# Sample tokens' attention to cached keys: 16 rows, transposed keys, scores inside the input projection; a fifth head's products one unit later

## The reference, cut to what matters

```python
def swa_sample(q, k, v, buf, window, dil):
    ...
    kk = jnp.concatenate([buf[:, :, 0].astype(F32), k.astype(F32)], axis=1)
    vv = jnp.concatenate([buf[:, :, 1].astype(F32), v.astype(F32)], axis=1)
    idx = Wb + jnp.arange(T)[:, None] - dil * jnp.arange(J + 1)[None, :]
    ...
    s = jnp.einsum('nthd,ntjhd->nthj', q.astype(F32), kg) * (Dh ** -0.5)
    mx = jnp.max(s, axis=-1, keepdims=True)
    p = jnp.exp(s - mx)
    den = jnp.sum(p, axis=-1)
    o = jnp.einsum('nthj,ntjhd->nthd', p, vg) / den[..., None]
    lse = mx[..., 0] + jnp.log(den)
# in mixer: the three groups are merged by their denominators
    alpha = jax.nn.softmax(jnp.stack(lses, axis=2), axis=2)
    out_s = (jnp.stack(outs, axis=2) * alpha[..., None]).reshape(B, T, W_SW)
```

## Time and profile before

| | |
|---|---|
| median of 3 runs | 2053.05 us (2052.51 to 2056.39) |
| the profiled execution, its own time | 2051.47 us |
| its span in the profile | 2049.7 us |
| PE, DVE, ACT, POOL busy | 1768.1, 990.9, 697.4, 361.9 us |
| layer 0: projection's last tile moved out, prompt's attention done, `window_end` | at 230.1, 271.5, 314.6 us |
| layer 1: the same three points | at 1111.2, 1151.4, 1197.0 us |

### The profile page before, as it was taken

One profiled execution on the slowest core, in us unless ns is written; L12 is line 12 of the kernel. 1 busy time (PEld: TensorE's weight loads), 2 busy tenths in 40 slices (PEclk: granted clock), 3 DMA queues, 4 the chain that ended last, 5 costly groups with the idle time before them and its releaser, 6 DMA issues. The chain is left out here.

```text
span 2049.7 us, 34030 instructions
## 1 busy us (share of the span) xinstructions
PE 1768.1 (86%) x13616; PEld 1652.8 (81%) x13616; DVE 990.9 (48%) x1485; ACT 697.4 (34%) x1038; POOL 361.9 (18%) x226
## 2 busy tenths in 40 slices
PE   6999846659999999997999567494999999999994
PEld 6898714449999999997997254394999999999994
DVE  4575463544221122226663735434664574574484
ACT  4443414214222122234333143134343353353342
POOL 4002401014344344441005000013000000000021
PEclk9999956569999999999999665596999999999997
DMA  4211306312222222222113010115876776786792
GB/s 169 73 63 52 115 0 235 134 46 83 86 91 96 77 87 93 99 77 73 63 53 125 0 62 0 45 64 214 278 242 236 269 257 227 258 276 217 249 332 68
DMA packets 68700, 270.71 MB, mean 132 GB/s; under 512 B 11189, under 2 KB 11925, under 8 KB 67773
## 3 DMA queue, kind: packets, MB, share of 16 engines
q1 hardware_dynamic: 61152, 242.05, 34.2%
q10 hardware_dynamic: 3772, 18.36, 2.6%
q0 software_dynamic: 3648, 8.53, 1.2%
HBM read 252.55 MB, written 36.29 MB: 141 GB/s over the span
## 5 line engine op out<-in xcount | busy, mean ns | idle before, releaser
L1651 PE MATMUL psum<-xg,xhi 128*128 128x320 f32 x1408 | 376.9, 310 | 0.9 <-issue 0.4
L1653 PE MATMUL psum<-xg,xlo 128*128 128x256 f32 x1408 | 375.3, 281 | 0.0
L1651 PEld LDWEIGHTS psum<-xg,xhi 128*128 128x128 f32 x1408 | 265.5, 189 | 2.9 <-issue 2.6
L583 POOL TENSOR_TENSOR wlo<-wraw,whi 128x1024 fp32r<-128x1024 f32 (+1 forms) x82 | 209.9, 2562 | 318.2 <-ACT whi L719 318.2
L1653 PEld LDWEIGHTS psum<-xg,xlo 128*128 128x128 f32 x1408 | 264.7, 188 | 0.0
L1122 PE MATMUL psum<-xnh,whi 128*128 128x260 f32 x1120 | 235.2, 292 | 31.1 <-POOL xnl L636 13.8
L719 ACT CAST whi<-wraw 128x1024 fp32r<-128x1024 f32 (+1 forms) x130 | 140.7, 1085 | 308.5 <-DMA wraw<-in_w_in 185.3
L403 DVE TENSOR_TENSOR xlo<-xraw,xhi 128x1024 fp32r<-128x1024 f32 x176 | 215.1, 1223 | 58.4 <-ACT xhi L1070 58.4
L1070 ACT CAST xhi<-xraw 128x1024 fp32r<-128x1024 f32 x176 | 182.9, 1049 | 148.3 <-PE psum L1653 148.2
L1122 PE MATMUL psum<-xnh,wlo 128*128 128x260 f32 x1120 | 229.9, 287 | 0.0
L1122 PE MATMUL psum<-xnl,whi 128*128 128x260 f32 x1120 | 229.9, 287 | 0.0
(11 more groups left out here) (434 smaller groups left out, 2629.7 us busy)
## 6 DMA issues: line engine op xcount, KB each, us to landing
xraw<-in_moe_gu SPq DMA_DIRECT2D x176, 512.0 KB, 4.1
xraw<-in_moe_dn SPq DMA_DIRECT2D x64, 704.0 KB, 6.0
wraw<-in_w_in SPq DMA_DIRECT2D x54, 512.0 KB, 3.2
wraw<-in_ffn_gu SPq DMA_DIRECT2D x44, 512.0 KB, 3.2
wraw<-in_ffn_dn SPq DMA_DIRECT2D x16, 704.0 KB, 4.1
wraw<-in_w_out SPq DMA_DIRECT2D x16, 512.0 KB, 3.3
out_cache_s<-in_cache SPq DMA_DIRECT2D x4, 2040.0 KB
a_ck<-in_ck ACTq DMA_DIRECT2D x2, 3072.0 KB, 11.3
```

The source lines that it names most:

```text
L583: pool.tensor_tensor(wlo[u % RAW][:, 0:cols], wraw[u % RAW][:, 0:cols], whi[u % SPL][:, 0:cols].bitcast(F32), ALU.subtract).then_inc(lo_ma ...
L1651: pe.matmul(epart(n), xhi[n % HIX][:, k * P:(k + 1) * P], xg[:, k, :], start=(k == 0), stop=False, skip_group_check=True)
L1653: ins = pe.matmul(epart(n)[:, 0:256], xlo[n % RWX][:, k * P:(k + 1) * P], xg[:, k, 0:256], start=False, stop=(k == KD - 1), skip_group_che ...
```

## The change

`a_ck`, the job groups `qb`, `sct`, `ppt` and `spv`, `osw` and the whole last part of `window` go. In their place:

- The cached keys come transposed, features on the partitions (`kt0` 128x8x129, `kt12` 128x8x82), the values as `cv` (128x8x2x128), together 1888 KB a layer in place of 3072 KB. ACT issues the three loads in its step 21, ahead of its squares, after waits for `qe_made` and `window_dma` of the layer before.
- Step 24 on DVE: one memset of `qm`, a wait for the loads, three copies of the own keys into the key tiles, six products that put each query into its own column, two columns (heads) a token.
- Step 25: PE makes the scores of all 8 tokens and 2 heads on 16 rows (`ws`: 24 products, weights `qm` 128x16, moving 129, 65 or 17 keys). DVE takes maxima, ACT four exponentials with sums, DVE the weights of the groups and the scaled probabilities `wp` (ten small instructions).
- Step 26: PE turns `wp` and spreads the own probabilities (`wp` job), ACT copies them to `pw`.
- In `window`: `tm` are two jobs instead of three; after the first scores PE makes `wv` (24 products, weights `cv` with 128 columns, moving 2 columns); DVE adds the own values in four small instructions between its maxima 3 and 4 and writes the result straight into `proj`.
- `fx` turns five blocks instead of eight, and DVE's copy of the other three goes.
- SP's wait for `window_end` ahead of the output projection's weights goes.
- At n = 9 PE makes heads 0 to 3; head 4 moves to n = 10, behind unit 10.
- `NLO` is 11: the low parts of units 7 to 10 are made by POOL.
- The wait for banks 4 to 7 ahead of `window` is now made job by job.

```diff
-NLO = 7
+NLO = 11
...
@@ ACT
+                    act.wait_ge(S("qe_made"), li + 1)
+                    act.wait_ge(window_dma, 112 * li)
+                    for name in ("kt0", "kt12", "cv"):
+                        act.dma_start(A[name][:], a[name][li]).then_inc(cache_in, 16)
                     for m in range(3):
...
+                elif n == 25:
+                    act.wait_ge(S("w_max"), li + 1)
+                    for g, (c0, c1, _) in enumerate(W_KEYS):
+                        ins = act.activation(A["wp"][:, c0:c1], bank("ws")[0:2 * NB, c0:c1], ACT.Exp, scale=0.125,
+                                             bias=A["snm"][:, g:g + 1], accum_out=A["sden"][:, g:g + 1])
...
+                    sig(act.activation(A["se"][:], A["se"][:], ACT.Exp, scale=0.125), "w_exp")
...
-                act.dma_start(A["ck"][:], a["ck"][li]).then_inc(cache_in, 16)
@@ PE
-                elif n == 9:
+                elif n in (9, 10):
...
-                    for heads in ((0, 1), (2, 3), (4,)):
+                    for heads in ((0, 1), (2, 3)) if n == 9 else ((4,),):
...
+                elif n == 25:
+                    pe.wait_ge(S("qm_made"), li + 1)
+                    j = Job(li, "ws")
+                    for g, (c0, c1, _) in enumerate(W_KEYS):
+                        for b in range(NB):
+                            j.mm(c0, c1 - c0, A["qm"][:, g, b].rearrange("p m h -> p (m h)"), window_keys(g, b),
+                                 start=(b == 0), stop=(b == NB - 1), rows=2 * NB)
+                    j.end()
...
                 scores(0)
+                pe.wait_ge(cache_in, 48 * (li + 1))
+                taken(pe, li, "wp")
+                j = Job(li, "wv")
+                for b in range(NB):
+                    c = 2 * b
+                    j.mm(c, 2, A["cv"][:, b, 0, :], A["pw"][:, c:c + 2])
+                    for g, (r, rows) in ((1, (0, 64)), (2, (64, 16))):
+                        j.mm(16 * g + c, 2, A["cv"][r:r + rows, b, 1, :], A["pw"][r:r + rows, 64 + c:66 + c])
+                j.end()
                 scores(1)
@@ DVE, end of window
-                step(v.memset(A["ss"][:], NEG))
-                step(tt(own, tms[:, 0:384], tms[:, 384:768], ALU.mult))
...
-                free(tt(osw[:], bank("spv")[0:NB, 0:384], own, ALU.add), li, "spv")
                 v.wait_ge(window_dma, 112 * (li + 1))
                 sig(v.memset(A["mx"][:], 0.0), "window_end")
@@ SP
-                sp.wait_ge(S("window_end"), li + 1)
```

More of the change, by code:

```diff
@@ L62, in mixer_jobs @@
 def mixer_jobs():
-    jobs = [("tm", i) for i in range(3)] + [("vt", g) for g in range(3)]
+    jobs = [("tm", i) for i in range(2)] + [("vt", g) for g in range(3)]
     def sc(n):
@@ L1731, in window @@
             def window(li):
-                for i in range(3):
+                for i in range(2):
                     made(v, li, "tm", i)
-                    cols = (4 if i < 2 else 1) * P
-                    free(v.tensor_copy(A["tms"][:, i * 512:i * 512 + cols], bank("tm", i)[0:NB, 0:cols]), li, "tm", i)
+                    free(v.tensor_copy(A["tms"][:, i * 384:i * 384 + 384], bank("tm", i)[0:NB, 0:384]), li, "tm", i)
                 def maxima(n):
@@ L1754, in weigh, with outputs @@
                     free(tt(natural(g, out), natural(g, lr[:, g, :]), grouped(g, bank("ld", g)[0:2, :]), ALU.mult), li, "ld", g)
-                for n in range(6):
+                def outputs(h):
+                    r = slice(64 * h, 64 * h + 64)
+                    own, out = (x.rearrange("p (g b h) -> p g b h", g=3, h=2)[r, :, :, h] for x in
+                                (A["pw"][:, 2 * NB:8 * NB], bank("wv")[:, 0:6 * NB]))
+                    step(tt(A["t8"][r], own, proj[r, TSV:TSV + 3, SEQ:T], ALU.mult))
+                    ins = tt(proj[r, TSQ:TSQ + 3, SEQ:T], out, A["t8"][r], ALU.add)
+                    if h:
+                        free(ins, li, "wv")
+                    else:
+                        step(ins)
+                for n in range(4):
+                    maxima(n)
+                made(v, li, "wv")
+                taken(v, li, "wp")
+                for h in range(2):
+                    outputs(h)
+                for n in range(4, 6):
                     maxima(n)
@@ L1808, in window @@
-                for g in range(3):
-                    rows = ROWS_G[g]
-                    made(v, li, "sct", g)
-                    free(v.tensor_copy(A["ss"][:, 2 * g:2 * g + 2, 0:rows],
-                                       bank("sct", g)[0:NB, 0:2 * P].rearrange("b (h s) -> b h s", h=2)[:, :, 0:rows]),
-                         li, "sct", g)
-                step(v.tensor_reduce(A["smx"][:], A["ss"][:], AX, ALU.max))
-                sig(tt(A["sp"][:], A["ss"][:], bc(A["smx"][:].unsqueeze(2), NB, 6, 129), ALU.subtract), "s_parts")
@@ L1831, in window @@
-                made(v, li, "ppt")
-                for g in range(3):
-                    rows = ROWS_G[g]
-                    ins = tt(A["pm"][0:rows, 2 * g:2 * g + 2, :, :].rearrange("p h n m -> p (h n) m"),
-                             bc(bank("ppt")[0:rows, 2 * g * NB:(2 * g + 2) * NB].unsqueeze(2), rows, 2 * NB, NB),
-                             K(C_DM, 2 * NB * NB, rows).rearrange("p (n m) -> p n m", m=NB), ALU.mult)
-                    if g < 2:
-                        step(ins)
-                    else:
-                        free(ins, li, "ppt")
```

211 lines of the change are left out of this document (98 added, 113 removed).

## The result

The changed kernel takes **1974.18 us** (median of 4 runs, 1973.61 to 1974.86), beside 2052.78 us for the kernel before (2050.28 to 2056.39): a ratio of 0.9619, with a 95% interval of 0.9606 to 0.9632, and 78.6 us less. The sum had promised 95.0. The profiled execution has a span of 1972.0 us in place of 2049.7, 77.7 less, at a mean granted clock of 0.903 in place of 0.889.

The account below looks back on a forecast made before the run. Bound: the DVE, PE and ACT chain ending `window`, elsewhere PE and the fifth head's wait. 88.5 + 1.0 + 18.3 - 7.2 - 3.6 - 2.0 = 95.0 us off 2053.05 gives 1958.0 us; range 1946 to 1974.

Parts of the forecast that it names:

- The chain: Cache attention at the end of `window`: removing its serial DVE, PE and ACT handovers gains 43.0 + 45.5 = 88.5 us.
- The values in `window`: 48 new PE instructions a layer at 92 ns, partly hidden by waits for ACT: 1.8 us a layer, 3.6 us lost.
- a rival at 1967: The clock falls at the new score or value products, costing some 4 to 5 us more a layer; chance 0.12.
- The fifth head and NLO: Own-position products: head 4 behind unit 10 no longer waits long, POOL's extra low parts covered; gain 18.3 us (15 to 20).
- part 2: The fifth head's term: 8.3 us gained in layer 0 and 10.0 us in layer 1, 18.3 us in all.
- stall that moved: Rival: the fifth head's stall only moves to another wait, giving back up to 18.3 us, 1976 us; chance 0.08.
- The condition that the prediction put on the clock there: Layer 1, fifth head: if a 2.8 us wait of PE lowers the clock, unit 11 costs some 3 us more.
- The scores: Step 25: 48 new PE instructions at full clock, 3.6 us a layer, cost 7.2 us in all.
- The softmax: Step 25: small DVE and ACT instructions take 4.8 us beside unit 26's 5.8; rival that they run longer, 1966 us, chance 0.08.
- Behind `window_end`: Start of `mlstm`: PE arrives without the dense small products before it, costing 1.0 us a layer, 2.0 us (0 to 4).
- the feared half clock: First product of `mlstm`: at half clock it would take 2 us more; half of that was counted a layer.
- `mlstm` did not speed up: Rival: PE gets full clock in `mlstm`, saving 14.9 us a layer, 29.7 in all, 1928 us; chance 0.04.

Follow-up runs that it names:

- w2: The changed kernel with its 24 value products a layer grouped by rows, all of 128, then 64, then 16: 1965.3 us, ratio 0.9584.
- w6: The changed kernel with 16 value products a layer, grouped by rows, a token's 64 and 16 rows merged into one product: 1959.4 us, ratio 0.9557.
- w1: The changed kernel with the window's value products made for one sample token only, 3 products instead of 24: 1961.8 us, ratio 0.9559.
- w10: The changed kernel with value products grouped by rows and operands exchanged, loading 2 probability columns and moving 128 value columns: 1965.1 us, ratio 0.9570.
- b2: The kernel before with only the fifth head's own-position products moved to unit 10, NLO = 7 as before: 2035.5 us, ratio 0.9924.
- w3: The changed kernel with NLO = 7, so POOL no longer makes the low parts of weights 7 to 10: 1971.4 us, ratio 0.9610.
- w5: The changed kernel with its value products grouped by rows and moved behind the window's three lm transposes: 1971.6 us, ratio 0.9607.
- w9: The changed kernel with NLO = 7 and 16 grouped value products, eight ahead of scores(1) and eight behind it: 1966.4 us, ratio 0.9584.
- w12: The changed kernel with NLO = 7 and 16 grouped value products at the window's end, all ahead of `al`: 1960.9 us, ratio 0.9547.

## Why the prediction was wrong

The time lies 0.2 us above the range, and 16 us above the number.

- **The chain (88.5 us): right.** `window_end` follows 0.07 us behind the last product, the stores were never waited for, and no other wait took the place.
- **The values in `window` (3.6 us): the step that failed.** It is short by some 12 us: from unit 26's move to the end of the prompt's attention it is 6.8 and 7.6 us longer than before, where 1 to 2 were foretold. Three things were wrong in it. The price of 92 ns came from ten instructions of the router in one piece of the chain, and not all ten are what the rows' heading says: eight load 128 columns, with starts 111 to 112 ns apart in the trace of before, and the last two, of the fifth block with its 8 tokens, load 8 columns. So the row was misread, and its own price for a load of 128 columns is 112 ns, which with equal rows throughout is what was measured (w2, w6). The products stand in the order 128, 64, 16 rows, which I had not priced, and that makes it 155. And the granted clock falls to half inside them and stays there for scores(1): I had that as a rival at 1967, with "against: they follow dense matmuls at full clock". The clock fell within 2.0 to 6.0 us of the first product in every run in which all of them are made and began at full clock, wherever they stood, though it falls near there in some runs without them too. In layer 0 these three make, worked out from the trace's steps, 48 x 0.112 = 5.4 us, 48 x 0.155 = 7.4 us, and the 9.5 us measured.

  The 2.6 us of waits for ACT that were to hide them hid little: 8.4 and 7.9 us of window go with seven eighths of them (w1).

  The figure of the Trainium skill ("TensorE: Matmul & The Clock Gate", section "LDWEIGHTS (loading the stationary operand)"), 107 ns a load whatever the rows, which I set aside for the row, is near what w2 and w6 measured at full clock (111 to 112). That section has no word for the mixed order or for the half clock's 213 to 284, and by its figure my estimate would have been 1.4 us longer. The remark beside it in the prediction, that it speaks against this operand order, isn't borne out: exchanged, a step is 109 ns (w10).
- **The fifth head and NLO (18.3 us): right in kind, 6 us too much.** The move alone gives 16.0 us (b2), so the working of part 2 was 2.3 too high, most of it in layer 1. The rest is the sentence "POOL pays for it": I asked when POOL would be done, which was in time, and not what it holds up meanwhile. That DVE's operations wait for POOL's, and what the clock does behind it, costs 3.6 us of trace (16.0 - 12.4), of which layer 1 has 3.0: the keys come late there, PE waits 5.14 us, and the four heads take 1.4 us more at half clock. Beside w3, where the clock fell in unit 11, it is only 2.1 us. This is no stall that moved, so that rival isn't what happened: with the head's move alone the four heads wait 2.15 us (b2), as before. The condition that the prediction put on the clock there was met: after a wait of 2.7 us it fell in w3 and not in b2, at 1.5 us for the 3 foretold.
- **The scores (7.2 us): right.** 3.24 us on PE for 3.6, and unit 25 to 26 is 9.12 us in both layers for the 9.4 foretold. Layer 0 lost 1.5 us more, in unit 22, with a clock of 0.66 from 195 to 200; some of the other runs had that stretch without it (w6 has 10.5 us from unit 21 to 22, the changed kernel 12.1). The softmax ended 0.27 us ahead of the tile's move, for 1 us foretold: a nearer thing than the sum made it.
- **Behind `window_end` (2.0 us): wrong in sign, small.** The two stretches behind it are 1.8 us shorter. In layer 0 the feared half clock did come, and the first product of `mlstm` took 1.8 us more than in the earlier trace rows:

```profile
283.03 3.84 PE L1190 MATMUL psum<-r_w,bd 128*128 128x260 f32 x8 [0.66 <-ACT r_w L901]
289.54 5.76 PE L1190 MATMUL psum<-r_w,bd 128*128 128x260 f32 x16 [2.67 <-ACT r_va L915]
```

  But the next wait for ACT shrank to 2.67 us, from 4.49 in the kernel before, and took it back. `mlstm` did not speed up: where the earlier trace rows have 0.50, the changed kernel has 0.50 too (1159 to 1167).

That the time is not further off is in part luck: the stretches of the last point gave 3.8 us more than foretold, for no cause that a run shows.

What remains open: why the clock falls. Narrow moving columns alone are not needed for it (w10), nor this place (w5), nor an uncut run (w9), nor, for a short fall, the products themselves (w12).

## What to carry to other kernels

Price many small products by their number, each with its load, in the order in which they stand, at both clocks, and put a chance of more than one in eight on the half clock when a price rests on the full one. Group products of equal rows and merge those that can share a load (24 to 16 was worth 5.5 us by the ratios; the grouping 7, of which 3.7 lie in the windows themselves). Before a price is taken from a short row, see whether all its instructions have the same shape. When work is given to POOL, ask not only whether it is done in time but which two-input operations of DVE stand beside it: each may be held up for as long as POOL's.

## What the runs showed of the hardware that I had not expected

- Instructions with a load of 128 columns and equal rows start 112 ns apart, and with rows of 128, 64, 16 in turn 155 on average (w2 and the changed kernel, full clock); 214 and 258 at half. A change of rows costs some 90 ns a product.
- POOL's clearing of `r_att` holds DVE up as well as its subtractions do. POOL's and DVE's timelines, changed kernel, layer 0:

```profile
78.80 2.24 POOL L619 MEMSET r_att<- 128x2560 f32 x1
```

```profile
78.82 3.04 DVE L1931 COPY r_kh<-r_w 128x1560 f32<-128x1560 f32 x1 [0.76 <-ACT r_w L816]
```

  The kernel before and w3 have this copy in 0.97 us; 81.04 + 0.97 would be 82.01, and it ends at 81.86.
- 24 products (48 instructions) that load 2 columns and move 128 have steps of 109 ns at full clock, against 112 for the same ones that load 128 and move 2 (w10 and w2). In layer 0 they take 5.7 us against 8.9, because w2's were mostly at half clock, and the clock still falls at their end.
